# A head's output products one chunk later in a hand-ordered recurrent layer with its FFN

## What is computed

```python
def step(s, blk):                       # gla_chunk_scan, per direction and head
    qc, kc, vc, gc = blk
    b = jnp.cumsum(gc, axis=-2)
    dec = _masked_exp(tri, b[..., :, None, :] - b[..., None, :, :])
    scores = jnp.einsum('...td,...sd,...tsd->...ts', qc, kc, dec)
    o = (jnp.einsum('...ts,...sv->...tv', scores, vc)
         + jnp.einsum('...td,...dv->...tv', qc * jnp.exp(b), s))
    s_new = (jnp.exp(b_end)[..., :, None] * s
             + jnp.einsum('...sd,...sv->...dv', kc * jnp.exp(b_end[..., None, :] - b), vc))
...
y_lat = _gated_out(_join_ways(o_l), g_l, o_norm, w_o)      # RMSNorm per head, * silu(g), @ w_o
h_lat = h_lat + m_lat[2] * y_lat
h_lat = h_lat + m_lat[5] * _swiglu(_modulate(_rms_norm(h_lat, norm_ffn[i]), m_lat[3], m_lat[4]), ...)
return _rms_norm(h_lat, final_norm)
```

## Time and profile before

| | us |
|---|---|
| median of 3 runs | 1879.26 (1879.11 to 1880.96) |
| the profiled execution, its own time | 1871.49 |
| its span, first to last instruction | 1869.7 |
| TensorE (PE) busy in it | 1817.2 |
| VectorE (DVE) busy | 1246.7 |
| ScalarE (ACT) busy | 886.4 |
| mean granted clock of TensorE | 0.994 of full |

### The profile page before, as it was taken

How to read it: one execution, slowest core, us unless ns; L and a number is a source line. 1 busy time by engine, 2 the same in 40 slices (tenths; PEclk the granted TensorE clock), 3 DMA queues, 4 the chain that set the end, 5 groups by cost and what they waited for, 6 DMA issues and landing times.

```text
span 1869.7 us, 27864 instructions
## 1 busy us (share of the span) xinstructions
PE 1817.2 (97%) x11295; PEld 1582.9 (85%) x11295; DVE 1246.7 (67%) x1935; ACT 886.4 (47%) x1224; POOL 0.2 (0%) x4
## 2 busy tenths in 40 slices
PE   8999999999999999998899989999999999999998
PEld 2278989898989898988899978888888888999996
DVE  6753878796979796979975565555555554444555
ACT  6762635353635454545554454444444444444444
POOL 0000000000000000000000000000000000000000
PEclk9999999999999999999999999999999999999999
DMA  9985545544444554444656546777677776555562
GB/s 372 366 271 157 173 132 161 159 155 124 150 143 140 154 160 138 142 140 143 218 168 227 183 123 214 234 231 228 214 228 232 224 234 206 175 185 182 182 184 96
DMA packets 175363, 352.94 MB, mean 189 GB/s; under 512 B 12738, under 2 KB 80643, under 8 KB 174595
## 3 DMA queue, kind: packets, MB, share of 16 engines
q1 hardware_dynamic: 175042, 351.11, 58.5%
q10 hardware_dynamic: 192, 0.05, 0.0%
HBM read 346.92 MB, written 4.19 MB: 188 GB/s over the span
## 4 chain that ended last, share of the span: by engine, by line
PE 81%; DVE 12%; issue 3%; ACT 2%; DMA 1%; ACTq 0%; DVEq 0%
PE bank L1162 10%; PE bank L1163 10%; PE bank L1164 10%; PE bank L1286 9%; PE bank L1288 9%; PE bank L1287 9%; DVE wlo L729 3%; PE bank L1177 2%; PE bank L1178 2%; PE bank L1179 2%; PE score L1342 2%; DVE work L904 2%; DVE aacc L825 2%; PE score L1162 2%; PE score L1163 2%
## 5 line engine op out<-in xcount | busy, mean ns | idle before, releaser
L729 DVE TENSOR_TENSOR wlo<-raw,whi 128x1024 fp32r<-128x1024 f32 x496 | 605.4, 1224 | 430.8 <-ACT whi L442 430.2
L442 ACT ACTIVATE whi<-raw 128x1024 fp32r<-128x1024 f32 x496 | 522.2, 1057 | 619.2 <-PE bank L1164 272.8
L1162 PE MATMUL bank<-ahi,whi 128*128 128x256 f32 (+1 forms) x1504 | 487.8, 324 | 6.2 <-DVE wlo L729 6.2
L1163 PE MATMUL bank<-alo,whi 128*128 128x256 f32 (+1 forms) x1504 | 481.6, 320 | 0.0
L1164 PE MATMUL bank<-ahi,wlo 128*128 128x256 f32 (+1 forms) x1504 | 481.5, 320 | 0.0
L1162 PEld LDWEIGHTS bank<-ahi,whi 128*128 128x128 f32 x1504 | 288.2, 192 | 26.5 <-DVE wlo L729 5.9
L1164 PEld LDWEIGHTS bank<-ahi,wlo 128*128 128x128 f32 x1504 | 287.9, 191 | 20.4
L1163 PEld LDWEIGHTS bank<-alo,whi 128*128 128x128 f32 x1504 | 288.2, 192 | 18.7
L1286 PE MATMUL bank<-whi,ahi 128*128 128x512 f32 x704 | 275.8, 392 | 2.8 <-DVE alo L1038 2.8
L1288 PE MATMUL bank<-whi,alo 128*128 128x512 f32 x704 | 274.5, 390 | 0.0
L1287 PE MATMUL bank<-wlo,ahi 128*128 128x512 f32 x704 | 274.4, 390 | 0.0
(11 more groups left out here) (226 smaller groups left out, 2134.8 us busy)
## 6 DMA issues: line engine op xcount, KB each, us to landing
raw<-in_w_ada_dram SPq DMA_DIRECT2D x168, 512.0 KB, 4.2
raw<-in_ffn_w_gate_dram SPq DMA_DIRECT2D x88, 512.0 KB, 4.3
raw<-in_ffn_w_up_dram SPq DMA_DIRECT2D x88, 512.0 KB, 4.4
raw<-in_ffn_w_down_dram SPq DMA_DIRECT2D x88, 512.0 KB, 3.7
raw<-in_hg_w_in_dram SPq DMA_DIRECT2D x128, 256.0 KB, 3.5
raw<-in_hg_w_f_dram SPq DMA_DIRECT2D x128, 256.0 KB, 3.5
raw<-in_hg_w_in_dram SPq DMA_DIRECT2D x32, 512.0 KB, 4.6
raw<-in_hg_w_o_dram SPq DMA_DIRECT2D x32, 512.0 KB, 3.7
```

The lines of the kernel that those rows point to most:

```text
L442: act.activation(whi[:, ck % SPL, :], raw[:, q % RAW, :], ACT.Copy).then_inc(s_hi, 1)
L729: dve.tensor_tensor(wlo[:, ck % SPL, :], raw[:, SEQ["w", ck] % RAW, :], whi[:, ck % SPL, :].bitcast(F32), ALU.subtract).then_inc(s_lo, 1)
L1162: pe.matmul(dst, w, ah, start=start, stop=False, skip_group_check=True)
L1163: pe.matmul(dst, w, al, start=False, stop=False, skip_group_check=True)
```

## The change

`tasks_at` and `tasks_tail` give steps 0 to 13 instead of 0 to 12. The output products go from step 9 to 10, the square and the mean-square product from 10 to 11, Ln and Exp from 11 to 12, the scaling from 12 to 13. Placing the second tokens' scores stays at step 9. In the stretched list of the last heads, products go from position 15 to 17 (head 14) and from 24 to 26 (head 15), the mean square from 17 to 18 and from 26 to 27, the scaling from 19 to 20 and from 28 to 29.

```diff
 def tasks_at(p, groups=True):
-    return [(p - s, off) for s, off in head_slots() if 0 <= p - s <= 12]
+    return [(p - s, off) for s, off in head_slots() if 0 <= p - s <= 13]
...
-        for j in range(13):
+        for j in range(14):
...
-                if j == 10:
+                if j == 11:
                     act.wait_ge(s_o, n + 1)
                     act.activation(osq, ob[:, 0:T], ACT.Square).then_inc(s_osq, 1)
-                if j == 11:
+                if j == 12:
                     act.wait_ge(s_om, n + 1)
...
-                if j == 12:
+                if j == 13:
                     dve.wait_ge(s_or, n + 1)
...
-                if j == 9:
+                if j == 10:
                     pe.wait_ge(s_pl, (2 * n + 2) * NL)
                     pe.wait_ge(s_s2, n + 1)
...
-                if j == 10:
+                if j == 11:
                     pe.wait_ge(s_osq, n + 1)
```

## The result

| | before | changed |
|---|---|---|
| median, us | 1879.18 (1877.4 to 1880.96, 4 runs) | 1861.04 (1859.31 to 1861.86, 4 runs) |
| ratio, 95% interval | | 0.9902 (0.9885 to 0.9919) |
| profiled execution, us | 1871.49 | 1859.31 |
| granted clock of the profiled one | 0.994 | 0.999 |

The profiled executions differ by 12.2 us. So most of the miss, some 6 of 7.1 us, is not between the two traces. It comes from the trace of before, which lies 7.7 us under its own median, while that of the changed kernel lies 1.7 us under its own.

A forecast was written before the change was run, and what follows sets the result against it. TensorE was taken to set the pace in the scan, VectorE in the output gate from 868 to 946 us. Terms 9.5 + 0.5 + 1.0 = 11.0 us gave 1860.5 profiled, plus 7.8 carried over: 1868.3 us, range 1863.5 to 1875.

The forecast's parts named there:

- term one: Scan, 120 to 850 us: TensorE's waits for VectorE's placing of scores go, -9.5 us.
- the visible waits: Scan: six waits of L1353 for VectorE's placing at L904, 8.4 us, all expected to go.
- the hidden ones: Scan: five waits showing only on TensorE's weight loads, 0.21 us each, 1.1 us; upper bound 3.1 us.
- Head 3's tight place: Scan, turning of head 3's keys: VectorE ends L951 0.8 us before TensorE starts L1324, the tightest place between points in step.
- The full stretch: Output gate, 868 to 946 us: VectorE sets the pace, so removing TensorE's two waits of 8.7 us gains nothing by itself.
- the forecast 0.5: Gate, copy at 946.33 us: VectorE waits less for ScalarE, -0.5 us, bounds nothing and 0.97.
- The last head: Head 15: L1360 no longer waits for the square behind the gate's table loads, -1.0 us, bounds nothing and 1.0.
- a rival of its own: Gate, behind the wait ending near 947 us: half-clock time comes back too, 1.5 us more, 1866.8 us; chance 0.18.
- ScalarE's order: Ln and Exp now precede the next head's exponentials: cost nothing, covered by 3.1 us; uncovered 0.9 us for each of 15 heads.
- SyncE: Fetch of x and output projection weights wait for the later last scaling: cost nothing, upper bound 2.9 us.
- The slack: Output projection: first weights land by 992 us, copied at 995.23; 3.2 us against a 2.9 us delay.
- the rule of the clock: Skill's rule that idle gaps between matmul bursts halve TensorE's clock; by it the sum would be 12.5 instead of 11.0 us.

The follow-up runs named there:

- the kernel with the later fetch: Changed kernel with SyncE's wait for the last scaling and the fetch of x three chunks further on in its list; 1860.47 us, ratio 0.9914.

## Why the prediction was wrong

*The waits of the scan, term one.* 9.4 us against 9.5 between the traces, and VectorE followed, but that the sum is right to the decimal is luck: two misses cancel. The prediction took the visible waits by their idle time and only the hidden ones by the distance between starts. Taken by that distance, head 3's wait is longer. Before, the last product ahead of it (the earlier trace rows has the waiting one, at 408.54 us):

```profile
405.95 0.28 PE L1179 MATMUL bank<-whi,alo 128*128 128x256 f32 x1
```

And in the changed kernel, at the same head's output:

```profile
412.12 0.28 PE L1179 MATMUL bank<-whi,alo 128*128 128x256 f32 x1
412.24 0.39 PE L1353 MATMUL ob<-work,arena 128*128 128x128 f32 x2
```

2.59 us between the starts against 0.12, so 2.47 and not 2.31, and 0.1 more behind it. For the six visible waits this makes 9.9 us instead of 8.4; the five hidden ones give 1.1, as forecast. From these 11.0 us the two new waits at L1177 take back 1.7 by the same measure, which the prediction had at nothing. Head 3's tight place did not shrink: its distance between L951 and L1324 grew from 0.8 to 1.2 us.

*The full stretch.* Right that the 8.7 us of waits are worth nothing there: from the gate's start to chunk 148 it is 95.7 us instead of 96.1, and the waits for wlo took their place, as foreseen. That these 0.5 us are the forecast 0.5 is not shown: the same stretch took 96.5 us in the second profile of the kernel before and 96.3 in the kernel with the later fetch, whose order there is the changed one.

*The last head and the clock in the gate.* From chunk 148 to the output projection it is 43.8 us instead of 46.5, 2.7 less. The second profile of the kernel before, whose clock was full there, took 45.2. So 1.3 us are the half clock from 947 us on the earlier trace rows, and 1.4 the new order, 0.4 above the prediction's bound of 1.0 for L1360; where the 0.4 lie is open. The clock was a rival of its own in the prediction (0.18); it came beside the forecast, not in its place.

*ScalarE's order.* Free, as forecast: no wait of L945 for L579. The Ln waits 1.8 us in all instead of 15.0. But the square of head 14 now stands behind the two table loads of the gate's L613 and L615, of 1.28 us each in the trace, and holds L1360 for 2.3 us, in the full stretch, where it costs nothing. I had placed that wait only at head 15.

*SyncE.* Forecast at nothing with an upper bound of 2.9 us; it was 0.6 by the wait of TensorE. The slack was put at 3.2 less 2.9 us, and the fetch took 9.0 us instead of 8.0.

**The step that failed** is the sentence behind the sum: "the median of the runs is 7.8 us above it, 1879.3, and I carry the difference over unchanged". That difference was itself lost clock, caused by the waits that the change removes. The second profile of the kernel before shows it (17 us at half clock behind waits of 2.3 us, 7.8 us in the scan), filling the waits takes 5.0 us away without shortening anything, one wait put back brings the clock of the runs down to 0.991 to 0.994, and the runs of the changed kernel stand at 0.996 to 0.999. What remains to be carried over is 1.7 us, not 7.8. The prediction had weighed the rule of the clock, and asked of the one trace whether it held: it said no for head 3's wait, because TensorE "ran on at full clock" there. In the next execution it did not. The sentence of the Trainium skill that it leaned on (TensorE: Matmul & The Clock Gate, section Why this matters for your kernels) is, besides, about gaps longer than 2.3 us, so it does not foresee this loss; here the measurement decides: in two traces the clock fell behind waits of 1.9 and 2.3 us. The clock should have been priced over the runs, whose median stood 0.4% above the profile with no other cause in sight. With 5 to 6 us more for the scan and 1.5 for the gate the forecast had been 1861 to 1862; this is reckoned afterwards, from the runs above.

## What to carry to other kernels

When the median of the timed runs lies above the profiled execution by more than their spread (here 7.8 us against 1.9 of the three runs), the trace in hand may be a lucky one: ask what the others lose, and whether the change touches it, before the difference is carried over. Where TensorE sets the pace, as in this scan, a wait costs its length plus what the clock does behind it; moving the consumer by one step of the program takes away both, and where no step is free, work of no use in the wait can take away the second. A wait of an engine that does not set the pace gives nothing when it is removed: TensorE's 8.7 us in the gate came back as waits for other things.

## What the hardware showed beyond that

The same program, with the same waits to within a hundredth of a microsecond, kept its clock in one execution and lost it for 10 and 7 us in the next. Four traces have two waits of 1.9 or 2.3 us each in the scan: in two of them the clock fell behind both, in two behind neither, and why is open. Over 42 timed runs of the kernel before, time and mean granted clock go together: 1879.0 us on average at 0.991 (11 runs), 1873.8 at 0.994 (4 runs). 0.003 of 1873 us is 5.6 us of TensorE's time at full clock, near the 5.2 us between them. The Trainium skill (TensorE: Matmul & The Clock Gate, section What's actually happening) says the watch on TensorE's activity runs freely and does not start with the kernel, and the spread from run to run agrees with it, though no run here tests it: a wait of 2.3 us behind which nothing happens in one execution costs several microseconds in another.
